# Odd heads of the latent attention: scores, transposes and last values one product earlier in TensorE's order

## The reference

```python
def mla_attention(c_q, c_kv, k_rope, q_a_g, kv_a_g, w_q_b, w_kv_b, cos, sin):
    q = (rmsnorm(c_q, q_a_g) @ w_q_b).reshape(b, s, MLA_HEADS, MLA_QK_DIM)      # 8 heads, 128 + 64
    q_nope = q[..., :MLA_NOPE_DIM]
    q_rope = rope(q[..., MLA_NOPE_DIM:], cos[:, None, :], sin[:, None, :])
    kv = (rmsnorm(c_kv, kv_a_g) @ w_kv_b).reshape(b, s, MLA_HEADS, MLA_NOPE_DIM + MLA_V_DIM)
    k_nope, v = kv[..., :MLA_NOPE_DIM], kv[..., MLA_NOPE_DIM:]
    k_r = rope(k_rope, cos, sin)
    ...
        sc = (einsum('bqhd,bkhd->bhqk', qn, k_nope) + einsum('bqhd,bkd->bhqk', qr, k_r)) * scale
        p = jax.nn.softmax(jnp.where(mask, sc, NEG), axis=-1)                    # causal
        return jnp.einsum('bhqk,bkhd->bqhd', p.astype(v.dtype), v)
```

## The kernel before

| product | what | matmuls | PSUM bank |
|---|---|---|---|
| 1 and 3 | query of the even head, its two weight chunks | 6 and 3 | 0 |
| 2 and 4 | rotary queries of both heads | 6 and 3 | 1 |
| 5 | key of the even head | 6 | 2 |
| 6 and 7 | values of both heads, half of the tokens each | 12 and 12 (256 columns) | 3, 0 |
| 8 and 9 | query of the odd head | 6 and 3 | 2 |
| 10 | key of the odd head | 6 | 3 |

## Time and profile before

### The profile page before, as it was taken

One profiled execution on the slowest core, in us unless ns is written; L12 is line 12 of the kernel. 1 busy time (PEld: TensorE's weight loads), 2 busy tenths in 40 slices (PEclk: granted clock), 3 DMA queues, 4 the chain that ended last, 5 costly groups with the idle time before them and its releaser, 6 DMA issues.

```text
span 2861.6 us, 33442 instructions
## 1 busy us (share of the span) xinstructions
PE 2760.5 (96%) x13124; PEld 2283.9 (80%) x13124; DVE 1352.3 (47%) x1882; ACT 996.3 (35%) x1557; POOL 1093.3 (38%) x536
## 2 busy tenths in 40 slices
PE   7999998899999999889999999999999999999997
PEld 5788887788888888778878887778878888888886
DVE  6756656833375665683354444454344222222323
ACT  5244434523324443553342333232223333333221
POOL 3443332234444433223433333333444444444442
PEclk9999998999999999999999999999999999999998
DMA  5342231235434223123542222222223333336333
GB/s 156 89 129 82 74 118 41 59 107 152 128 95 129 74 76 122 43 62 103 148 124 82 68 71 76 74 74 75 88 87 109 113 111 113 114 111 213 111 125 110
DMA packets 307612, 289.13 MB, mean 101 GB/s; under 512 B 33153, under 2 KB 256001, under 8 KB 306945
## 3 DMA queue, kind: packets, MB, share of 16 engines
q1 hardware_dynamic: 300656, 264.46, 31.1%
q10 hardware_dynamic: 6800, 22.55, 2.0%
HBM read 260.19 MB, written 26.74 MB: 100 GB/s over the span
## 4 chain that ended last, share of the span: by engine, by line
PE 76%; DVE 16%; ACT 4%; issue 2%; POOL 1%; DMA 1%; SPq 0%; DVEq 0%; ACTq 0%
PE bank L832 22%; PE bank L834 22%; PE bank L833 22%; DVE probs L1611 2%; PE work L1051 1%; DVE pt L1619 1%; DVE act_in L1184 1%; POOL w_lo L823 1%; PE o_bank L832 1%; DVE probs L1585 1%; ACT w_hi L682 1%; PE o_bank L833 1%; PE o_bank L834 1%; DVE stat L1578 1%; DVE mixed L1385 1%
## 5 line engine op out<-in xcount | busy, mean ns | idle before, releaser
L823 POOL TENSOR_TENSOR w_lo<-w_raw,w_hi 128x1024 fp32r<-128x1024 f32 (+3 forms) x468 | 1007.2, 2155 | 1481.9 <-ACT w_hi L682 1481.9
L832 PE MATMUL bank<-act_in,w_hi 128*128 128x512 f32 x2664 | 1056.0, 396 | 34.5 <-DVEq L1227 13.2
L834 PE MATMUL bank<-act_in,w_lo 128*128 128x512 f32 x2664 | 1042.6, 391 | 0.0
L833 PE MATMUL bank<-act_in,w_hi 128*128 128x512 f32 x2664 | 1041.4, 391 | 0.0
L682 ACT ACTIVATE w_hi<-w_raw 128x1024 fp32r<-128x1024 f32 (+3 forms) x468 | 437.8, 938 | 1070.0 <-PE bank L834 642.8
L832 PEld LDWEIGHTS bank<-act_in,w_hi 128*128 128x128 f32 x2664 | 502.2, 189 | 143.4 <-POOL w_lo L823 20.4
L834 PEld LDWEIGHTS bank<-act_in,w_lo 128*128 128x128 f32 x2664 | 501.7, 188 | 107.7
L833 PEld LDWEIGHTS bank<-act_in,w_hi 128*128 128x128 f32 x2664 | 502.6, 189 | 99.1 <-issue 1.4
L832 PE MATMUL bank<-mixed,w_hi 128*128 128x512 f32 x768 | 299.5, 390 | 0.2 <-POOL w_lo L823 0.2
L834 PE MATMUL bank<-mixed,w_lo 128*128 128x512 f32 x768 | 298.8, 389 | 0.0
L833 PE MATMUL bank<-mixed,w_hi 128*128 128x512 f32 x768 | 298.8, 389 | 0.0
(11 more groups left out here) (267 smaller groups left out, 2820.7 us busy)
## 6 DMA issues: line engine op xcount, KB each, us to landing
w_raw<-in_w_in SPq DMA_DIRECT2D x512, 128.0 KB, 2.4
w_raw<-in_w_in SPq DMA_DIRECT2D x224, 256.0 KB, 2.9
w_raw<-in_w_out SPq DMA_DIRECT2D x64, 512.0 KB, 3.7
w_raw<-in_w_in SPq DMA_DIRECT2D x32, 512.0 KB, 3.7
w_raw<-in_w_out SPq DMA_DIRECT2D x64, 256.0 KB, 4.6
probs<-in_xT SPq DMA_DIRECT2D x32, 256.0 KB, 4.9
x_scr<-buf ACTq DMA_DIRECT2D x32, 256.0 KB, 3.2
probs<-x_scr SPq DMA_DIRECT2D x32, 256.0 KB, 5.0
```

The source lines that it names most:

```text
L823: nc.gpsimd.tensor_tensor(lo, raw, hi, ALU.subtract).then_inc(lo_ready, 1)
L832: pe.matmul(dst, lhs[0], rhs[0], start=start, stop=False, skip_group_check=skip)
L833: pe.matmul(dst, lhs[0], rhs[1], start=False, stop=False, skip_group_check=skip)
L834: return pe.matmul(dst, lhs[1], rhs[0], start=False, stop=stop, skip_group_check=skip)
```

## The change

Each odd head's scores and `mla_norm` fall due after product 3 instead of 4 of the next pair, its transposes after 6 instead of 7. Its values stay after product 8. For the last pair (`i == 3`) the same holds in the output projection, and there the values come after product 9 instead of 10. Outputs stay where they are.

```diff
         if kind == "mla1":
-            head("mla", l, 2 * i + 1, 0, [(4, "mla_scores"), (4, "mla_norm"), (7, "transpose"),
-                                          (8 if i < 3 else 10, "values"), (12, "output")])
+            head("mla", l, 2 * i + 1, 0, [(3, "mla_scores"), (3, "mla_norm"), (6, "transpose"),
+                                          (8 if i < 3 else 9, "values"), (12, "output")])
```

## The result

The changed kernel takes 2890.95 us (2885.29 to 2891.52, 4 runs) against 2862.27 us: a ratio of 1.0093, 95% interval 1.0080 to 1.0105, or about 27 us slower by the ratio. The profiled execution has a span of 2889.9 us, 28.3 us longer. The forecast of 2882 us had the direction, and the time lies within the range; the loss is 1.4 times the 19.4 us of the sum.

What follows compares the result with a forecast made beforehand. VectorE was taken to bound the latent attention stage. Queue order 14.6 us, last heads 2.8 and clock 2 sum to 19.4 us on the profiled 2863.2 us; less 0.8 us to the median, 2882 us, range 2867 to 2893.

Steps and rivals of the forecast that it cites:

- VectorE sets the pace here: First layer's latent attention: VectorE is the bound, and TensorE's gaps are its slack.
- Norm and rotary read change places: VectorE, odd heads inside pairs: norm first, product 5's read 9.4 us behind scaling; `pt` 2.1 us later (head 3); sum 14.6 us.
- Scores one product earlier: TensorE, three odd heads per layer: product 4 goes from before the scores to behind them; gain 0.
- A stall of about 3 us before product 8: TensorE in the next pair: product 8 waits about 3 us for product 5's read, the next scores 0.3 us.
- The last head: Output projection: scores wait 3.8 us instead of 2.41, nothing takes the product's place; 1.4 us per layer, 2.8 us.
- The clock: Scores behind four new stalls before heads 4 and 6: 1 us each for two, 2 us; bounds 0 and 12 us.
- the clock doubles the damage: Rival, 14%: same mechanism, all four new scores blocks at half clock, 3.1 us each exposed; 2892 us.

Runs made afterwards that it cites:

- busy stall: Six odd heads inside pairs moved, last head left, and product 7 of the pairs they fall into computed three times; 2888.26 us, ratio 1.0091 to the kernel before.
- TensorE's order alone: Against the kernel before, TensorE alone has six odd heads' scores after product 3; transposes after 6 on all engines, last head left; 2880.61 us, ratio 1.0065.
- only the pairs moved: Against the kernel before, scores, norm and transposes moved only for the odd heads that fall into a next pair; last head left; 2886.08 us, ratio 1.0089.

## Why the prediction was right in direction and short in size

- *VectorE sets the pace here.* Right. Cutting its rotary read took 20 us off the kernel before, and moving only the transposes changed nothing for the better.
- *Norm and rotary read change places, 9.4 us from scaling to read, 2.1 us later for head 3.* Right in its path, and in its size where no cast is hindered: 9.4 us and 2.1 us in the kernel with the busy stall. In the changed kernel it was 9.8 to 9.9 us in all six places, for a rotary cast took 0.97 us instead of 0.42. GpSimd subtracts the chunk of product 10 at that moment (the cast from 517.12), and the rotary read now lies where the chunks are split. I had no term for that. It is the first part of the miss: 17.6 us on this path instead of 14.6.

```profile
517.06 0.72 POOL L823 TENSOR_TENSOR w_lo<-w_raw,w_hi 128x256 fp32r<-128x256 f32 x1 [1.71 <-ACT w_hi L682]
```

- *Scores one product earlier, gain 0, cost 0.* Wrong. I gave the whole 14.6 us to the queues' order and took product 4 as fill. The run with TensorE's order alone shows that product 4 behind the scores is enough for 18.6 us, and the swaps on ScalarE and VectorE add the rest to 25. It isn't free at head 1 either. There the same product stood in front of a wait, which grew from 2.2 to 2.9 us. In layer 1 the scores behind it took 6.6 to 6.9 us in all seven traces with the longer wait. In the seven with the shorter one they took 3.9 us six times and 5.45 us once. That is 3.0 us that the sum had at nothing. No run changes this wait alone.
- *A stall of about 3 us before product 8, 0.3 before the scores.* 4.01 and 0 for head 4: the transposes came earlier and the read later than I had them.
- *The last head, 2.8 us.* Too large at the middle: 1.4 us with an interval that holds both 0 and 2.8. "Nothing takes the product's place" missed that the conversion's new time frees a cast of VectorE.
- *The clock, 2 us.* **The term that was sized worst.** Of the 25.1 us between heads 1 and 7, the 17.6 us of VectorE's path leave 7.5 us, the 3.0 at head 1 among them; my bound was 12. These 7.5 us are a remainder, and that slow blocks fill it is argued from where they lie. In the changed kernel nine of the fourteen scores blocks from head 1 on are over 4.7 us long, and before it was five. The prediction named heads 1 and 2 of layer 0 as the slow ones and overlooked head 2 of layer 1 and head 7 of both layers (5.5 us each). It counted new slow blocks only behind four new stalls; there were six stalls, and heads 1 and 5 to 7 of layer 1 were slow or partly slow too (6.88, 5.47, 4.44 and 7.05 us). Which block falls slow also differs between traces that are alike in that place: head 7 of layer 0, behind a wait of 2.4 us, took 5.47 us in the kernel before and 3.90 us with only the pairs moved. So the share of one place can't be read from one trace.

The forecast's rival "the clock doubles the damage" stands nearest: 2892 us. That is partly luck. It put 12.4 us on the clock, where 7.5 are left at most, and the hindered casts, which it did not have, fill 3 us of the difference. The cause that it names shows in the stage with the busy stall, with 3.3 us, and not in the whole time.

## What to carry to other kernels

When one list orders all engines, moving a step past a product also moves everything that this product feeds. Look for the longest read behind that product and for what used to hide the hand-over to it, before counting matmuls as cover. A step that waits longest may be harmless: ask what shares its queue, and if a wait is to be filled from behind, move every step that would then stand first (the even head's values here). Where VectorE sets the pace, cover on TensorE bought nothing here, and each new stall of TensorE may be paid a second time in its clock.

## What the runs showed of the hardware

A VectorE cast of 512 columns took 0.43 us alone and 2.23 us beside a GpSimd subtraction of 2.37 us, ending 0.28 us behind it; the norm's four scalings took 1.28 and 3.44 us likewise. The Trainium skill, "SBUF — State Buffer", section "Terms", says that VectorE and GpSimd share a port pair which one holds exclusively for a whole instruction. The trace agrees for these two: the scalings too ended 0.28 us behind GpSimd's instruction. Four ScalarE copies of 32 rows took 0.59 us each, as long as one of 128 rows and the same 512 columns (0.58 to 0.61 us), so splitting by rows cost three copies, and these stood on the chain here.
